# RWKV-7 scan on one Trainium2 core: value products moved ahead of the scan and into its waits, in a bank of their own, and VectorE's side work put at fixed places

## What is computed

```
def step(S, inp):
    r_t, w_t, k_t, v_t, aa_t, bb_t = inp
    sa = jnp.einsum('bhvk,bhk->bhv', S, aa_t)
    S = S * w_t[:, :, None, :] + sa[..., None] * bb_t[:, :, None, :] + v_t[..., None] * k_t[:, :, None, :]
    y_t = jnp.einsum('bhvk,bhk->bhv', S, r_t)
    return S, y_t
```

## Time and profile before

| | us |
|---|---|
| median of 3 runs (lowest to highest) | 1110.15 (1109.57 to 1110.42) |
| profiled execution, span from the first to the last instruction | 1108.2 |
| PE busy | 1087.0 (98%) |
| DVE busy | 683.1 (62%) |
| ACT busy | 504.8 (46%) |
| POOL busy | 92.1 (8%) |

### The profile page before, as it was taken

One profiled execution on the slowest core, in us unless ns is written; L12 is line 12 of the kernel. 1 busy time (PEld: TensorE's weight loads), 2 busy tenths in 40 slices (PEclk: granted clock), 3 DMA queues, 4 the chain that ended last, 5 costly groups with the idle time before them and its releaser, 6 DMA issues.

```text
span 1108.2 us, 17971 instructions
## 1 busy us (share of the span) xinstructions
PE 1087.0 (98%) x6744; PEld 852.3 (77%) x6744; DVE 683.1 (62%) x1171; ACT 504.8 (46%) x865; POOL 92.1 (8%) x149
## 2 busy tenths in 40 slices
PE   7999999999999999999999999999999999999997
PEld 6887888767677777777767888888888888888886
DVE  4224665688878878787777444457677767752234
ACT  5426556634534445244543333465556555631122
POOL 8100001111010110101110010100000000000000
PEclk9999999999999999999999999999999999999999
DMA  8632332310111111111323544433333333322221
GB/s 216 131 94 77 95 95 78 95 39 20 39 39 49 47 50 58 49 59 41 113 71 102 149 138 132 122 105 95 95 95 95 95 95 95 95 96 95 96 76 77
DMA packets 154391, 97.02 MB, mean 88 GB/s; under 512 B 30761, under 2 KB 143575, under 8 KB 154327
## 3 DMA queue, kind: packets, MB, share of 16 engines
q1 hardware_dynamic: 148800, 79.72, 25.1%
q0 software_dynamic: 5376, 16.37, 4.9%
q10 hardware_dynamic: 151, 0.04, 0.0%
HBM read 87.71 MB, written 8.39 MB: 87 GB/s over the span
## 4 chain that ended last, share of the span: by engine, by line
PE 83%; DVE 8%; issue 5%; DMA 1%; ACT 1%; SPq 1%; DVEq 0%; ACTq 0%
PE ps L1661 15%; PE ps L1664 15%; PE ps L1663 15%; PE ps L1617 4%; PE ps L2162 4%; PE ps L2160 4%; PE ps L2161 4%; PE ps L1619 3%; PE ps L1618 3%; DVE wlo L1110 2%; PE ps L1947 2%; PE ps L1926 1%; PE ps L1882 1%; DMA raw<-in_w_in 1%; PE ps L1859 1%
## 5 line engine op out<-in xcount | busy, mean ns | idle before, releaser
L1110 DVE TENSOR_TENSOR wlo<-raw,whi 128x1024 fp32r<-128x1024 f32 x142 | 173.6, 1223 | 211.5 <-ACT whi L703 139.4
L703 ACT ACTIVATE whi<-raw 128x1024 fp32r<-128x1024 f32 x124 | 131.1, 1057 | 128.1 <-PE ps L1664 121.0
L1661 PE MATMUL ps<-xnh,whi 128*128 128x512 f32 x344 | 135.8, 395 | 0.0
L1664 PE MATMUL ps<-xnh,wlo 128*128 128x512 f32 x344 | 135.7, 395 | 0.0
L1663 PE MATMUL ps<-xnl,whi 128*128 128x512 f32 x344 | 135.7, 395 | 0.0
L1661 PE MATMUL ps<-xh,whi 128*128 128x512 f32 x248 | 99.8, 402 | 2.3 <-DVE xl L1128 1.7
L1664 PE MATMUL ps<-xh,wlo 128*128 128x512 f32 x248 | 97.9, 395 | 0.0
L1663 PE MATMUL ps<-xl,whi 128*128 128x512 f32 x248 | 97.8, 394 | 0.0
L1617 PE MATMUL ps<-xh,whi 128*128 128x512 f32 x184 | 88.7, 482 | 0.0
L1664 PEld LDWEIGHTS ps<-xnh,wlo 128*128 128x128 f32 x344 | 64.8, 188 | 15.2
L1663 PEld LDWEIGHTS ps<-xnl,whi 128*128 128x128 f32 x344 | 64.8, 188 | 15.1
(11 more groups left out here) (348 smaller groups left out, 2185.5 us busy)
## 6 DMA issues: line engine op xcount, KB each, us to landing
raw<-in_w_in SPq DMA_DIRECT2D x108, 256.0 KB, 3.2
raw<-in_w_up SPq DMA_DIRECT2D x88, 256.0 KB, 3.1
raw<-in_w_down SPq DMA_DIRECT2D x44, 256.0 KB, 2.9
gates_scratch<-gst POOLq DMA_DIRECT2D x16, 256.0 KB, 2.4
raw<-in_w_proj_b SPq DMA_DIRECT2D x16, 256.0 KB, 4.1
raw<-in_w_proj_a SPq DMA_DIRECT2D x16, 256.0 KB, 3.1
gl<-gates_scratch POOLq DMA_DIRECT2D x16, 256.0 KB, 3.0
raw<-in_w_out SPq DMA_DIRECT2D x16, 256.0 KB, 3.1
```

The lines of the kernel that those rows point to most:

```text
L703: act.activation(flat(whi[:, hb]), flat(raw[:, b]), ACT.Copy).then_inc(w_hi, 1)
L1110: dve.tensor_tensor(flat(lo[:, hb]), flat(raw[:, b]), flat(hi[:, hb]).bitcast(F32), ALU.subtract).then_inc(w_lo, 1)
L1661: pe.matmul(ps[bank][:, :], whi[:, hb, k, :], hi(k), start=first and k == 0, stop=False)
L1664: ins = pe.matmul(ps[bank][:, :], wlo[:, hb, k, :], hi(k), start=False, stop=last and k == kn - 1)
```

## The change

On TensorE: the value products of chunk 0 (both heads, bank 4) are issued in `invert`, behind L1900 and ahead of the "remainder" fill, with the wait for bank 4 moved along. Those of chunks 1 to 3 go to bank 0, which the inverse has left by then: chunk 1's two ahead of chunk 0's btok product; of chunks 2 and 3 one head ahead of the btok product of the chunk before and one behind it. The output part "v" of chunk 0 is issued in chunk 1 with "u". On VectorE: the copy zp of chunk 0 runs at the end of `invert`, right behind xf; the pieces have fixed places (`("first",)` ahead of chunk 0's up, `(j, "z")`, `(j, "u")`, `(j, "s")` behind the copies of chunk j); b_hat stands behind chunk 3's zp and k_hat behind its up; weights(N_FILL + 3n) moves from inside the scan to behind it. In scan 7 no piece stands between zp and up.

```diff
@@ VectorE, end of invert
+                dve.wait_ge(z_ps, 2 * (n * NT + 1))
+                dve.tensor_copy(zp[:, :], ps[4][:, 0:P]).then_inc(z_ready, 1)
@@ VectorE, scan
-                for j in range(NT):
-                    dve.wait_ge(z_ps, 2 * (d * NT + j + 1))
-                    dve.tensor_copy(zp[:, :], ps[4 + j % 2][:, 0:P]).then_inc(z_ready, 1)
-                    fill()
+                fill("first")
+                for j in range(NT):
+                    if j:
+                        dve.wait_ge(z_ps, 2 * (d * NT + j + 1))
+                        dve.tensor_copy(zp[:, :], ps[0][:, 0:P]).then_inc(z_ready, 1)
+                        fill(j, "z")
@@ VectorE, loop over pairs
-                prep = prepare(n)
-                scan(n - 1, prep[:2] + [lambda: weights(N_FILL + 3 * n)] + prep[2:])
+                key, rates, factor, modified, removed, a_tilde, r_tilde, b_hat, k_hat = prepare(n)
+                scan(n - 1, {("first",): [key], (0, "u"): [rates], (0, "s"): [factor],
+                             (1, "u"): [modified], (1, "s"): [removed], (2, "u"): [a_tilde],
+                             (2, "s"): [r_tilde], (3, "z"): [b_hat], (3, "u"): [k_hat]})
+                weights(N_FILL + 3 * n)
                 fill_low(3 * n - 1)
@@ VectorE, scan 7
-            scan(PAIRS - 1, [lambda: weights(N_PROJ + 1), lambda: add_bonus(PAIRS - 1),
-                             lambda: y_lo(0, 0, 3), lambda: y_lo(0, 1, 4), lambda: y_lo(0, 2, 5),
+            scan(PAIRS - 1, {("first",): [lambda: weights(N_PROJ + 1)],
+                             (0, "u"): [lambda: add_bonus(PAIRS - 1)],
+                             (0, "s"): [lambda: y_lo(0, 0, 3)],
+                             (1, "u"): [lambda: y_lo(0, 1, 4)],
+                             (1, "s"): [lambda: y_lo(0, 2, 5)],
...
@@ TensorE, invert, behind L1900
+                pe.wait_ge(ps_free, N_FILL + 3 * n + 2)
+                for h in range(2):
+                    hs = slice(h * HD, (h + 1) * HD)
+                    pe.matmul(ps[4][:, hs], gk[:, 0, h, 0:C], vp[:, 0, hs], start=True, stop=True)\
+                        .then_inc(z_ps, 1)
                 fill("remainder")
@@ TensorE, scan
-                pe.wait_ge(ps_free, N_FILL + 3 * d + 2)
+                zb = ps[0][:, 0:P]
+                def chunk_values(j, h):
+                    pe.matmul(zb[:, heads[h]], gk[:, j, h, 0:C], vp[:, j, heads[h]], start=h == 0,
+                              stop=False)
                 for j in range(NT):
-                    zb, ub = ps[4 + j % 2][:, 0:P], ps[5 - j % 2][:, 0:P]
-                    for h, hs in enumerate(heads):
-                        ins = pe.matmul(zb[:, hs], gk[:, j, h, 0:C], vp[:, j, hs], start=h == 0 or j == 0,
-                                        stop=j == 0)
-                        if j == 0:
-                            ins.then_inc(z_ps, 1)
+                    sb_, ub = ps[4 + j % 2][:, 0:P], ps[5 - j % 2][:, 0:P]
                     if j:
                         fill((j, "state"))
...
-                        output(j - 1, "u" if j == 1 else "vsu")
-                    else:
-                        output(0, "v")
+                        output(j - 1, "vu" if j == 1 else "vsu")
...
                         if j:
-                            pe.matmul(zb, ident[:, :], stm[:, j % 2, :], start=True, stop=False)
-                        pe.matmul(zb, ktok[:, j, :], vp[:, j, :], start=j == 0, stop=False)
+                            pe.matmul(sb_, ident[:, :], stm[:, j % 2, :], start=True, stop=False)
+                        pe.matmul(sb_, ktok[:, j, :], vp[:, j, :], start=j == 0, stop=False)
+                        chunk_values(j + 1, 0)
+                        if j == 0:
+                            chunk_values(1, 1)
...
                     pe.wait_ge(u_ready, d * NT + j + 1)
                     if j < NT - 1:
-                        pe.matmul(zb, btok[:, j, :], up[:, j % 2, :], start=False, stop=True)\
+                        pe.matmul(sb_, btok[:, j, :], up[:, j % 2, :], start=False, stop=True)\
                             .then_inc(s_ps, 1)
+                        if j:
+                            chunk_values(j + 1, 1)
```

More of the change, by code:

```diff
@@ L1373, in invert, with fill @@
                         ps[2 * g][:, :], ALU.mult, ALU.add).then_inc(xf_ready, 1)
+                dve.wait_ge(z_ps, 2 * (n * NT + 1))
+                dve.tensor_copy(zp[:, :], ps[4][:, 0:P]).then_inc(z_ready, 1)
             def scan(d, pieces):
[L1377 to L1381, removed]
+                def fill(*place):
+                    for piece in pieces.get(place, ()):
+                        piece()
+                fill("first")
                 for j in range(NT):
-                    dve.wait_ge(z_ps, 2 * (d * NT + j + 1))
-                    dve.tensor_copy(zp[:, :], ps[4 + j % 2][:, 0:P]).then_inc(z_ready, 1)
-                    fill()
+                    if j:
+                        dve.wait_ge(z_ps, 2 * (d * NT + j + 1))
+                        dve.tensor_copy(zp[:, :], ps[0][:, 0:P]).then_inc(z_ready, 1)
+                        fill(j, "z")
                     dve.wait_ge(u_ps, 2 * (d * NT + j + 1))
                     dve.tensor_copy(up[:, j % 2, :], ps[5 - j % 2][:, 0:P]).then_inc(u_ready, 1)
-                    fill()
+                    fill(j, "u")
                     if j < NT - 1:
@@ L1394, in scan @@
                                                  ALU.mult, ALU.mult).then_inc(s_ready, 1)
-                        fill()
-                for piece in pieces:
-                    piece()
+                        fill(j, "s")
             def y_lo(t, i, order):
@@ L1463, in y_lo_of @@
                 lo_part(dst, src, hi, yl_ready, 1)
-            scan(PAIRS - 1, [lambda: weights(N_PROJ + 1), lambda: add_bonus(PAIRS - 1),
-                             lambda: y_lo(0, 0, 3), lambda: y_lo(0, 1, 4), lambda: y_lo(0, 2, 5),
-                             lambda: y_lo_of(flat(ybl[:, 6:8]), flat(q67), flat(ybh[:, 6:8]), 6),
-                             lambda: y_lo_of(yal[:, 6, :], z[:, 6, :], yah[:, 6, :], 7)])
+            scan(PAIRS - 1, {("first",): [lambda: weights(N_PROJ + 1)],
[3 more added lines that the diff above has]
+                             (1, "s"): [lambda: y_lo(0, 2, 5)],
+                             (2, "u"): [lambda: y_lo_of(flat(ybl[:, 6:8]), flat(q67),
+                                                        flat(ybh[:, 6:8]), 6)],
+                             (2, "s"): [lambda: y_lo_of(yal[:, 6, :], z[:, 6, :], yah[:, 6, :],
+                                                        7)]})
             y_lo(1, 0, 0)
```

## The result

The changed kernel takes 1101.28 us (median of 5 runs, 1100.17 to 1101.51), where the kernel before, in five runs beside it, takes 1110.15 (1109.57 to 1111.37). The ratio is 0.9918, with a 95% interval of 0.9907 to 0.9928. It is faster by 8.9 us; 1102.1 had been forecast.

A forecast was written before the change was run, and what follows sets the result against it. TensorE was taken to bound the kernel. Scans 1 to 6 gain 6.3 us, scan 0 0.4 and the last 1.3, sum 8.0: 1110.15 - 8.0 = 1102.1 us, range 1100.4 to 1106.4.

The forecast's parts named there:

- The bound: Whole kernel: TensorE, busy 1087 of 1108.2 us, sets the end; a microsecond off its scan queue leaves the span.
- The waits only move: Rival: time won in scans returns as TensorE's waits for VectorE's masks and inverse, all 8 us: 1110; chance 0.08.
- Part 1: Chunk 0's z products ahead of the inverse's last fill: 0.14 to 0.15 us paid, xf products 0.74 earlier.
- Part 2: Chunk 1's value products fill the wait for up: btok 1.15 us behind xf products; head gains 1.00 in all.
- Part 3: Output part "v" (0.27 us) hides in chunk 1's 0.37 wait for zp; fill to next xf products stays 1.65.
- Part 4: Chunks 2 and 3: value products split around btok, 0.185 us each; 0.05 gained a scan, stm 0.1 spare.
- Scan 0 and the last scan: First and last of eight scans: gains of 0.4 us (0.3 allowed for masks) and 1.3 us.
- Part 5: VectorE's k_hat and subtraction moved to the scan's end: 0.56 us spare before the first mask; POOL's later product costs nothing.
- Products set between others: Rival, the slower side: lone value products take 0.275 us a record instead of 0.093, giving 1113.9; slower 0.06.
- POOL ahead of the subtraction: Rival: POOL's product holds VectorE 1.27 us, masks 0.7 late, 4.2 us in six pairs: 1106.3; chance 0.08.
- The unhidden z products: Rival: moved z products hide nothing, 0.23 to 0.25 us more in each of eight scans: 1104.1; chance 0.14.
- It gains more: Rival: zp without the subtraction before it, btok without small waits, 0.1 to 0.25 us a scan: 1101; chance 0.08.

The follow-up runs named there:

- no_xf_wait: The changed kernel without TensorE's own wait for xf at the scan's head: 1106.09 us in a single run, pair 45.31.
- split_all: The changed kernel with chunk 1's second value product behind btok as well, so all three chunks are split: 1101.36 us in a single run, pair 45.28.
- v_old_place: The changed kernel with the first output part "v" back in chunk 0, ahead of the xf products: 1103.6 us, pair 45.60.
- both_behind: The changed kernel with both value products of the next chunk behind btok in every chunk: 1105.25 us in a single run.
- both_ahead: The changed kernel with both value products ahead of btok in every chunk: 1101.65 us in a single run, pair 45.44.
- pool_first: The changed kernel with a 0.48 us clear on VectorE between k_hat and the weight subtraction: 1102.15 us, pair 45.33.
- weights_inside: The changed kernel with the weight subtraction inside the scan again, between chunk 0's stm and chunk 1's zp: 1104.43 us, pair 45.77.

## Why the prediction was right, point by point

**The bound** held. TensorE's queue sets the end, and what left it in a scan left the span: 8.9 us of gaps and starts, with PE at 98% in both kernels. "The waits only move" did not come: L1867's wait is 5.3 us beside 5.2.

**Part 1** held in mechanism and was 0.1 too good. The z products' place costs 0.14, as worked out, and the second group of L1921 has no gap. zp starts 1.20 behind xf (391.34 - 390.14), as forecast. The error is in the last step: I took zp's start to the xf products as 0.34 and got 0.43 (391.34 to 391.77). So TensorE waits 0.16 behind the end of the fills where 0.05 was said, and xf products come 0.63 earlier, not 0.74. Before, zp to the products was 0.34 with four output products in front of them; here they follow a fill. Why this step is 0.09 longer is not settled; no_xf_wait rules out the separate wait for xf.

**Part 2** was right up to btok and 0.14 too dear behind it. xf products to btok took 1.14 (391.77 to 392.91; 1.15 forecast). Btok to the fill took 0.19, not 0.33, so xf products to the fill are 1.33 and not 1.48. I had priced btok from a row where value products followed it and where its load had waited for up.

**Part 3** failed by 0.19: the fill to the next xf products is 1.84, not 1.65, outside my bounds. 0.09 of it lies ahead of the state product (0.86 instead of 0.77) and 0.1 between it and the xf products (0.98 instead of 0.88). Most of both is the late stm: in split_all, where stm is in time, the two are 0.78 and 0.90, and the whole is 1.68. "v" keeps 0.02 to 0.03 of the 0.19; with the late stm it costs 0.07 (v_old_place). I had called "v" hidden because its 0.27 is less than the idle 0.37 of row 398.97. But 0.17 of such a gap stands in chunks 2 and 3 as well, where zp is in time. By the starts the room was 0.26: from output "u" to the xf products it was 0.57 in chunk 1 of the kernel before (398.40 to 398.97) and 0.31 in its chunk 2 (402.36 to 402.67). Parts 2 and 3 together gave 0.22 where 0.26 was forecast.

**Part 4** is the term that was mis-sized. Forecast was 0.05 for chunks 1 and 2; they gave 0.38 (0.22 and 0.16). I priced a value product at 0.185 wherever it stands, so moving it could bring only the small waits of btok, which I put at 0.06 in chunk 1 and at nothing in chunk 2. Between ktok and btok it adds 0.12 to their distance (0.28 before, 0.40 after), and the one behind btok brings the stretch from btok to the fill to 0.41, where two made 0.69 (0.33 and 0.36). both_behind puts 0.15 a chunk back, and both_ahead keeps it.

That btok "doesn't" wait in chunk 2 was a misreading. It is not in the list of waits, but its load starts 0.05 behind the end of up, and its record is the long one:

```profile
403.37 0.29 DVE L1388 COPY up<-ps 128x128 f32<-128x128 f32 x1 [0.36 <-PE ps L1947]
...
403.71 0.30 PEld L1957 LDWEIGHTS ps<-up,btok 128*128 128x128 f32 x2
```

So the chain through up set btok in all chunks of the kernel before, and the value product ahead of it now covers that. An estimate from these rows puts 0.05 to 0.1 of each 0.15 down to it: 0.06 behind btok, and 0 to 0.05 ahead, as a product that waits for nothing starts 0.22 to 0.27 behind its neighbour there. The remainder is not explained.

The 0.1 spare for stm was taken up, as Part 3 shows.

**Scan 0 and the last scan.** Scan 0 gave 0.75 where 0.4 was forecast. Of the 0.3 for head products that "come on top", 0.07 came: chunk 1 to 2 takes 3.34 instead of 3.33, chunk 2 to 3 3.33 instead of 3.27. The 0.3 allowed for its masks was put in the wrong place. They are 0.28 late, as forecast (first mask 1.46 behind the scores instead of 1.18), but they stand behind the scores that end this stretch. They cost about 0.15 in the next one: the last products of the inverse start 0.57 later after the scores than before, where it is 0.42 in the pair behind, and that pair's gain is 1.03 and not 1.19. The last scan gave 1.28; 1.3 was forecast.

**Part 5** held in what it cost and not in why. VectorE is ready before the first mask in the steady pairs, which stands at 1.18 behind the scores. In pair 2 the piece of `fill_low` takes the spare up without passing it (1.17), and pool_first shows that 0.48 us more there is paid for. The subtraction had been treated as a piece that may stand anywhere; weights_inside shows that its old place would have cost 0.46 a pair in the new scan, for ScalarE's half is only done at 395.46. And POOL's product, put down as "nothing", grew by 0.85 us in seven pairs; it still cost nothing, for its result is wanted only in the inverse.

**The rivals.** Products set between others pay no latency; the four cost less in such places than side by side behind btok, and this rival (1113.9) falls by its own row: ktok, value, btok, value, fill stand 0.23, 0.17, 0.27 and 0.14 apart. POOL ahead of the subtraction (1106.3) falls by pool_first, as far as POOL's records tell when it starts. The unhidden z products (1104.1) fall by the closed gap, though the xf products come 0.11 later than forecast, by the step from zp. "It gains more" was right in its size of 0.1 to 0.25 a scan, and named the small waits of btok as one source; they were larger than I had read them, and the rest of the gain in chunks 1 and 2 came with the order.

The Trainium skill (SBUF — State Buffer, the section on the doors into SBUF) says that two such operations take a shared port pair in turn, the later one blocked until the first has ended. The trace agrees that they don't run side by side: POOL's record grows by 0.85 to 1.32 us beside a subtraction of 1.16 to 1.22, and is 1.27 in weights_inside, where none stands beside it. That the later one is the one blocked is not what these rows show: in pool_first POOL's record began first, and it was POOL's that grew. A record's start need not be the start of its reads, so they don't refute it either.

By scan, the forecast of 1.05 was 0.15 too high in the head (0.11 in Part 1, 0.04 in Parts 2 and 3) and 0.33 too low in chunks 1 and 2, and the pairs gained 1.15 to 1.21 (the first 1.03). That the number came out only 0.8 us from the forecast is in part luck, as these errors partly cancel.

## What to carry to other kernels

Price a short product by the distance between the starts of its neighbours in the very order that it will have, not by its share of a group elsewhere: the same products took 0.96 or 0.81 here. Look for a wait in the rows and not only in the list of waits: a load that starts right behind the end of the copy that it reads is waiting, though no idle time is named. When products are moved into a wait, look at the next hand-over (here stm, with 0.1 us spare), for the gain may be given back there: chunk 0 gained 0.41 from the xf products to the fill and lost 0.19 behind it. And judge a local change by its own stretch in the trace: 0.1 us a pair repeats there, while some 5 us of variation ahead of the scans hide it in the total.

## What the runs showed of the hardware

- POOL's product of two operands in SBUF takes 1.27 us with no such subtraction beside it, 2.12 beside a VectorE subtraction of two operands in SBUF that starts 0.23 before it, and 2.59 where its record starts 0.30 before the subtraction (and during a clear). VectorE's took 1.22 and 1.16. In none of these VectorE's was the one to grow.
- A float32 product of 64 columns (two records) added 0.12 us between a product that reads ready data and btok, and 0.14 as the last one before a fill; four records of such products behind btok took 0.36 to the fill, and btok to them 0.33, where btok to a fill took 0.19. A part of what makes the new order cheaper is a wait for up that it covers; the rest is open, as no run separated the weight loads from the change of bank and operand.
- Where a weight load waited for VectorE's copy it started 0.05 to 0.06 behind the copy's end (btok in chunks 0 to 2 of all eight scans of the kernel before; in chunks 1 and 2 of the loop scans the list of waits has no entry for it). The matmul behind it then had the longer record (0.49 instead of 0.44), and the next product stood 0.32 to 0.33 behind instead of 0.27 to 0.28.
- From the last output product to the xf products it is 0.31 to 0.32 in chunks 2 and 3, with 0.17 of idle weight load and no engine named. In chunk 1 of the changed kernel the same 0.32 and 0.17 stand there with zp named.
- A wait that is named for one engine's operation can belong to the next on that engine: with the wait for xf taken out, TensorE's weight load was idle for the same 0.41 us.
